# Norm scale and residual of a channel mixer applied once, in the last quarter, and VectorE's sums and low parts at group switches put in another order

## What is computed

```
hmlp = jax.nn.relu(rmsnorm(x, norm_mlp) @ w_up)
x = x + (hmlp * hmlp) @ w_down
...
y_prompt = rmsnorm(xp, norm_final)
```

## Time and profile before

| | |
|---|---|
| median of 3 runs | 2247.58 us (2243.97 to 2250.3) |
| the profiled execution: time, span | 2242.76 us, 2241.0 us |
| PE busy | 2157.6 us (96% of the span) |
| DVE busy | 1519.6 us (68%) |
| POOL busy | 1154.0 us (51%) |
| ACT busy | 667.8 us (30%) |

### The profile page before, as it was taken

How to read it: one execution, slowest core, us unless ns; L and a number is a source line. 1 busy time by engine, 2 the same in 40 slices (tenths; PEclk the granted TensorE clock), 3 DMA queues, 4 the chain that set the end, 5 groups by cost and what they waited for, 6 DMA issues and landing times.

```text
span 2241.0 us, 37284 instructions
## 1 busy us (share of the span) xinstructions
PE 2157.6 (96%) x14230; PEld 2129.1 (95%) x14230; DVE 1519.6 (68%) x1578; ACT 667.8 (30%) x850; POOL 1154.0 (51%) x785
## 2 busy tenths in 40 slices
PE   7999999999999999999999998979999999898998
PEld 6999999999999999999999998979999999898988
DVE  6576767165757667676757546477777678988856
ACT  4443434113223232323232202232222242433322
POOL 4556555342424334243424334458777778787761
PEclk9999999999999999999999999999999999999999
DMA  3212113421211112121212124423434554434322
GB/s 123 67 58 66 58 57 104 148 95 39 76 59 52 55 47 64 43 68 43 64 47 74 33 87 133 128 82 118 158 118 154 182 199 167 149 106 126 114 62 81
DMA packets 88609, 207.53 MB, mean 93 GB/s; under 512 B 8880, under 2 KB 14128, under 8 KB 87504
## 3 DMA queue, kind: packets, MB, share of 16 engines
q1 hardware_dynamic: 62992, 132.58, 18.8%
q10 hardware_dynamic: 25536, 73.83, 9.6%
HBM read 157.03 MB, written 49.34 MB: 92 GB/s over the span
## 4 chain that ended last, share of the span: by engine, by line
PE 76%; DVE 14%; issue 6%; ACT 3%; DMA 1%; DVEq 0%; POOL 0%; POOLq 0%; ACTq 0%; SPq 0%
PE ps L808 43%; PE ps L1031 21%; PE ps L1130 4%; DVE vt L1708 2%; PE ps L929 2%; DVE acc L1711 2%; DVE form_lo L1711 2%; PE ps L957 1%; DVE tmp L1711 1%; PE ps L975 1%; PE ps L978 1%; DVE snap L1711 1%; ACT vt L1140 1%; DVE xm_lo L1711 1%; PE ps L983 1%
## 5 line engine op out<-in xcount | busy, mean ns | idle before, releaser
L686 POOL TENSOR_TENSOR w_hi<-w_raw,ones 128x512 fp32r<-128x512 f32 x218 | 267.6, 1228 | 831.7 <-PE ps L808 803.6
L808 PE MATMUL ps<-u_hi,w_hi 128*128 128x364 f32 x1560 | 348.1, 331 | 16.9 <-POOL w_lo L689 9.6
L689 POOL TENSOR_TENSOR w_lo<-w_raw,w_hi 128x512 fp32r<-128x512 f32 x218 | 348.8, 1600 | 17.1
L808 PE MATMUL ps<-u_hi,w_lo 128*128 128x364 f32 x1560 | 344.8, 329 | 0.0
L808 PE MATMUL ps<-u_lo,w_hi 128*128 128x364 f32 x1560 | 344.3, 329 | 0.0
L808 PEld LDWEIGHTS ps<-u_hi,w_hi 128*128 128x128 f32 x1560 | 271.1, 189 | 19.4 <-issue 10.7
L808 PEld LDWEIGHTS ps<-u_lo,w_hi 128*128 128x128 f32 x1560 | 271.7, 188 | 0.0
L808 PEld LDWEIGHTS ps<-u_hi,w_lo 128*128 128x128 f32 x1560 | 271.6, 188 | 0.0
L1031 PE MATMUL ps<-form_hi,hi 128*128 128x274 f32 x784 | 168.9, 298 | 28.6 <-DVE small L1711 17.0
L1031 PE MATMUL ps<-form_hi,w_hi 128*128 128x274 f32 x776 | 164.0, 293 | 6.2 <-DVE small L1711 5.8
L1031 PE MATMUL ps<-form_lo,hi 128*128 128x274 f32 x784 | 167.5, 296 | 0.0
(11 more groups left out here) (286 smaller groups left out, 4510.9 us busy)
## 6 DMA issues: line engine op xcount, KB each, us to landing
w_raw<-in_w SPq DMA_DIRECT2D x290, 256.0 KB, 2.6
stage<-hid_forms SPq DMA_DIRECT2D x42, 548.0 KB, 3.9
rstd<-in_w SPq DMA_DIRECT2D x42, 256.0 KB, 2.6
hid_forms<-acc ACTq DMA_DIRECT2D x12, 822.0 KB, 6.6
bc<-out_rows ACTq DMA_DIRECT2D x8, 1092.0 KB, 6.1
hid_forms<-stage ACTq DMA_DIRECT2D x6, 1096.0 KB, 4.4
hid_forms<-acc ACTq DMA_DIRECT2D x6, 1096.0 KB, 4.4
acc<-in_x_t SPq DMA_DIRECT2D x8, 546.0 KB, 8.0
```

The costliest lines, as they stand in the source:

```text
L686: nc.gpsimd.tensor_tensor(w_hi[:, c, :], w_raw[:, c, :], one, ALU.mult).then_inc(s_whi, 1)
L689: nc.gpsimd.tensor_tensor(w_lo[:, c, :], w_raw[:, c, :], w_hi[:, c, :].bitcast(F32), ALU.subtract).then_inc(s_wlo, 1)
L808: mm = nc.tensor.matmul(slots[slot][:, t, :], w, r(k)[:, t * TW:(t + 1) * TW], start=(k == 0 and n == 0), stop=(k == last_k and n == 2))
```

## The change

The diff, cut to its core:

```diff
-ADDS = 8
+ADDS = 4
...
+    rings = [tmp[:, 2, 0:LAST_W], tmp[:, 2, LAST_W:2 * LAST_W], small[:, 0:LAST_W]]
...
+    def ring(q):
+
+        n = 2 * FORMS * DOWN_GROUPS + KB + q
+        return rings[n % STAGES], h_in[n % STAGES], 16 * (n // STAGES) + 16
...
-        def residual(first):
-            sp.dma_start(acc[:, first:first + 4, :], x2_d[first:first + 4].rearrange("j p c -> p j c"))\
-                .then_inc(g_in[first // 4], 16)
-
...
                 if q >= LAST_BANKS:
-                    pe.wait_ge(f_prod, q - LAST_BANKS + 1)
+                    pe.wait_ge(f_prod, 2 * (q - LAST_BANKS) + 1)
...
+        def residual(q):
+
+            lo, hi = LAST_TILES[q // KB]
+            dst, inc, count = ring(q)
+            act.dma_start(dst[:, 0:hi - lo], x2_d[q % KB, :, lo:hi]).then_inc(inc, 16)
+
+        act.wait_ge(o_st, 16 * KB)
+        act.wait_ge(v_lo, PRODUCTS)
+        act.wait_ge(h_add, ADDS * 4 * (DOWN_GROUPS - 1))
+        for q in range(STAGES):
+            residual(q)
 
         def final(t, n):
             lo, hi = LAST_TILES[t]
             q = KB * t + n
             act.wait_ge(f_acc, q + 1)
+            if q + STAGES < KB * TILES:
+                residual(q + STAGES)
...
-            if r == 3 and step == 3 and v <= DOWN_GROUPS:
-                staged_lo(v, B22)
...
-            if r == 0 and step == 0 and v > 1:
-                staged_lo(v - 1, T4)
+            if v <= DOWN_GROUPS:
+                f = {(2, 5): B11, (3, 0): T1, (3, 1): T2, (3, 3): B21, (3, 4): T3}.get((r, step))
+                if f is not None:
+                    staged_lo(v, f)
+            else:
+                first = {(2, 5): 0, (3, 0): 2, (3, 1): 4, (3, 2): 6}.get((r, step))
+                if first is not None:
+                    last_lo(first)
+            if v > 1 and r == 0 and step in (1, 2):
+                staged_lo(v - 1, (B22, T4)[step - 1])
...
+        def direct(group, r, product, n, half, part, count, over):
+
+            mm_done(group, r, product)
+            dve.wait_ge(s_q, QUARTERS * (4 * group + r) + max(count, over))
+            tt(as2(acc[:, n, (FIRST, SECOND)[half]]), bank(group, r, product), as2(part), ALU.add, s_q)
...
-            tt(tmp[:, 2, lo:hi], ps[:, q % LAST_BANKS, 0:hi - lo], tmp[:, 3, lo:hi], ALU.mult, f_prod)
-            dve.wait_ge(f_prod, q + 1)
-            tt(acc[:, n, lo:hi], acc[:, n, lo:hi], tmp[:, 2, lo:hi], ALU.add, f_acc)
+            x2, inc, count = ring(q)
+            y = acc[:, n, lo:hi]
+            tt(y, ps[:, q % LAST_BANKS, 0:hi - lo], y, ALU.add, f_prod)
+            dve.wait_ge(f_prod, 2 * q + 1)
+            tt(y, y, tmp[:, 3, lo:hi], ALU.mult, f_prod)
+            dve.wait_ge(f_prod, 2 * q + 2)
+            dve.wait_ge(inc, count)
+            tt(y, y, x2[:, 0:hi - lo], ALU.add, f_acc)
```

More of the change, by code:

```diff
@@ L2240, in partials @@
             mm_done(group, r, P6)
+            if isinstance(group, int) and group >= UP_GROUPS:
+                dve.wait_ge(s_q, QUARTERS * u)
             dve.wait_ge(s_snap, u + 1)
@@ L2370, in _ @@
             partials(group, r)
+            operands(group, r, 1)
             for stored_hid, count in hid_free(group, r):
@@ L2389, in mixer_add @@
                 tt(acc[:, n, FIRST], acc[:, n, FIRST], part, ALU.add, h_add)
[L2390 to L2398 removed]
+            dve.wait_ge(h_add, ADDS * (u - 4 * UP_GROUPS - 4) + done)
@@ new lines, in _ @@
+        group = UP_GROUPS
+        for r in range(4):
+            u = 4 * group + r
+            operands(group, r, 0)
+            partials(group, r)
+            for j in range(2):
+                dve.wait_ge(h_st[j], 32 * 6 + (32 if r >= 2 else 0))
+            operands(group, r, 1)
+            direct(group, r, P2, 2 * r, 0, snap1[:], 2, 0)
+            operands(group, r, 2)
+            direct(group, r, P7, 2 * r + 1, 1, snap4, 2, 0)
+            quarter(group, r, P7, snap2[:], snap2[:], 1)
+            operands(group, r, 3)
+            direct(group, r, P3, 2 * r, 1, snap4, 2, 3)
+            operands(group, r, 4)
+            direct(group, r, P4, 2 * r + 1, 0, snap2[:], 5, 4)
+            operands(group, r, 5)
```

65 lines of the change are left out of this document (17 added, 48 removed).

## The result

The changed kernel takes 2252.84 us in the median of 20 runs (2248.66 to 2259.62); the kernel before, beside it, 2245.15 us in 20 runs (2238.6 to 2250.3). The ratio is 1.0033, 95% interval 1.0026 to 1.0041: slower by 7.7 us, just above the 6.7 us that the prediction took as the least that can be told from no change. The profiled execution of the changed kernel has a span of 2249.8 us, 8.8 us more than before's 2241.0, and the same mean granted clock, 0.987. VectorE (DVE) is busy 1447.6 us instead of 1519.6 and POOL 1120.7 instead of 1154.0: 72 and 33 us of their busy time are gone, and the kernel is slower.

What follows compares the result with a forecast made beforehand. PE, busy 96% of the span, was taken as the bound. Stops +3.1, clock +0.8, POOL +3.0 and tail +1.9 sum to +8.8 us: 2247.6 + 8.8 = 2256.4 us on the median, range 2239.5 to 2267.

Steps and rivals of the forecast that it cites:

- (a): Likeliest, chance 0.45: stops move from r=3 to next group's start, last quarter pays; +9 us, +4 to +14.
- Stops in r = 3: Before P1 in units 15, 19, 23, 27: all four PE stops vanish, giving back 17.0 us.
- New stop before P1: In r=0 at units 16, 20, 24: PE waits 5.0 us each, 15.0 in all, for 5.3 before.
- New stop before P6: In r=0: PE stops of 3.3 (unit 16), 1.4 (20) and 4.2 us (24), 8.9 in all.
- Before the last quarter: PE's stop ahead of the last quarter grows to 2.5 us, for 0.9, as block 4's low part moves later.
- Stops together: Net of PE's new stops, less the 23.3 us of stops before the change: +3.1 us.
- Low clock: PE's stretches at the lower clock behind stops, five before, cost 0.8 us more.
- POOL in the first tile: Last quarter's first tile: POOL, meeting a third DVE instruction and starting later, costs PE 3.0 us (0 to 4.5).
- Tail: Last five blocks: one more 0.35 us DVE instruction each delays the last sum of squares, +1.9 us.
- (b): Rival, chance 0.15: the chain into P6 is hidden at the group switches; -2.6 us, no measurable change.
- (c): Rival, chance 0.18: every link of the chains at its low end; -8.0 us, 2239.6.
- (d): Rival, chance 0.22: links at their high end, landings 4.6 and more, longer P1 and P6 stops; +18 us, 2265.6.

Runs made afterwards that it cites:

- The two experiments on two links: Changed kernel with B22's low part back in r = 3: 2234.78 us; changed kernel with ACT's rounding of T4 moved later: 2234.86 us.
- e8: Changed kernel with ACT's rounding of T4 at step 2, B21's low parts a step earlier, T3's at step 3, B22's at step 5: 2226.67 us.
- the quarter alone: Changed kernel with the low parts in the old order, so only the last quarter's scale and residual are new: 2234.77 us.
- the order alone: Kernel before with only the new order of low parts; multiplications, additions and residual as before: 2268.89 us.
- e7: Changed kernel with most low parts at old places, T2's at r = 3 step 2, T4's later, ACT's rounding of T4 at step 2: 2227.14 us.

## Why the prediction was right

It said +8.8 us, 2256.4 on the median of the three runs shown; the medians differ by 7.7 and the spans by 8.8. The likeliest case, (a), holds, within its range, and the mechanism it named, stops that move from r = 3 to the start of the next group, is in the trace. That the spans differ by just 8.8 is luck: the stops came out 2.3 us lower than its sum, clock, POOL and tail 1.0, 1.1 and 1.0 higher, and -0.8 lies where it had no term.

- **Stops in r = 3, 17.0 us go**: they went, all four.
- **New stop before P1, 5.0 us each, 15.0**: 4.42, 4.29, 4.67, in all 13.4. Every link was where the prediction put it. The mis-sized ones, in unit 20: B22's first low part 1.25 us, not 1.8 and below the lower bound of 1.45, beside a POOL that stood idle there (7.69 us before 1952.33); T4's second half 3.85 us from issue to ACT's rounding, not 4.1. The two experiments on two links show the chain.
- **New stop before P6, 8.9 in all (3.3, 1.4, 4.2)**: P5 and P6 together 2.76, 0.23 and 5.25, in all 8.2. In unit 16 it stands before P5 and not P6: ACT waited 4.30 us for B21's second half, whose slot T2's first low part frees (also moved behind the partial sums), and P5's weights are queued behind it. The prediction followed only the chain to P6. In unit 24 the place is right. ACT's timeline there, T3's second half and then the copy:

```profile
2033.90 1.12 ACT L1134 ACTIVATE form_hi<-stage 128x1096 fp32r<-128x1096 f32 x1 [3.91 <-DMA stage<-hid_forms]
2034.93 0.61 ACT L1134 ACTIVATE snap<-ps 128x548 f32<-128x548 f32 x1
```

  Its slot was freed by B21's first low part, 2.3 us (4.59 for two from 2028.12), the high bound; the load took 3.5 us, inside the bounds. What B21's place costs is shown by e8: with it one step earlier, the stop is 1.02.
- **Before the last quarter 2.5**: 2.24, with 0.17.
- **Stops together +3.1**: +0.8, 2.3 too high. **Low clock +0.8**: +1.8. I had costed the clock by the number of stretches, and they are five as before; but the two at unit 24 cost 2.5 and 2.9 us, the other three 1.6 to 1.7. (The prediction's own terms for before, 1.7 + 2.1 and three of 1.7, make 8.9, not its 8.6; measured 8.5.)
- **POOL in the first tile +3.0 (0 to 4.5)**: +4.1 in these two executions, of the size given, but mis-split. The prediction put most of it on the third instruction and "some" on the late start. Against the kernel before, POOL starts 4.0 us later beside PE (3.5 us ahead, not 7.5), runs 1.2 us longer, and 1.0 us of slack behind its last chunk is gone; its 28 instructions took 38.4 us and 38.8 before. The 17.3 us for six chunks, from which it had POOL losing ground to PE, hold 1.3 us of waiting for transfers; without them a block's two chunks take 5.3 us of POOL, less than PE's 5.59. Other pairs give the instruction some part: 1.3 to 1.8 us by the medians, 2.2 by the profiles (48.75 against 46.55), 1.0 for the quarter alone (45.66 against 44.63), whose POOL starts 6.7 us ahead; the order alone, with the late start and without the instruction, has 47.16. Since two executions of one kernel differ by 2.5 us here, the split is argued, not shown. POOL's 28 instructions took 2.6 us more than without the instruction. The estimate by the exclusive lock of the Trainium skill's "SBUF — State Buffer", "Who interferes with whom", was 4.8 us, that by partial overlap 0 to 3.2, and the second is the nearer here.
- **Tail +1.9**: +2.9. The mechanism is shown (the same kernel without that instruction has 24.27 us, and the kernel before 24.26), the size was short by 1.0. The five instructions of 0.38 are there. The prediction counted only these. Ahead of them the tile's first blocks are late too: the stop of 0.46 us at the second norm and block 19's own third instruction put the reciprocal 13.57 us behind the tile's first matmul where it was 12.48, and ACT's square of the last block comes 0.3 us later (0.46 against 0.16 of waiting). That the transfers are hidden holds for all but one: block 16's, the last tile's first, is 0.83 us late, and the running sum behind it is what the second norm waits for. All the kernels with three instructions in that block have such a wait of 0.7 to 0.8 us and a stop of 0.3 to 0.5 at the second norm; the two kernels without the addition have neither.

The rivals: (b) fails because the P5 and P6 stops are 8.2 us; its reason against, late landings in bursts, holds (3.5/4.4/8.1 us min, median and max after, 3.4/4.1/7.9 before). (c) needed all links low: B22's was, B21's was not. (d) needed landings of 4.6 and more at P1; in unit 20 it was 3.9. What the prediction did not see is how much lay in the other half: it took no separate term for what the 74 us off DVE shorten, and the last quarter alone is a gain of 12 us, the order a loss of 18 in its presence and 22 without it.

## What to carry to other kernels

When an instruction is moved behind a wait, follow what its completion starts on other queues: here a stage slot, a load, a rounding, and the weight copies queued behind it in ScalarE's order. It was not the moved 2.5 us of VectorE's work that cost, but the 10 us from P6's end to P1's weights, and an edit on ScalarE, not on VectorE, undid the loss as well.

Time the halves of a change apart before judging it: 12 us gained and 18 lost look like a small loss. And ask of a stop not only how long it is but what clock follows: 24 us of stops brought 10 us of low clock with them, 12 to 13 us brought 3.3 to 8.0, and 7 to 8 us of shorter ones brought from none to 3.4.

When two engines feed one stage, look which of them sets its end before a longer stage is called slower: the first tile is 2.5 us shorter in the profile of e7 in which TensorE comes to it 2.0 us later, and ends at the same time.

Work placed ahead of time belongs where the engine waits for its producer, block by block, not where it is already behind: one block's behind each block of the middle tile, it lost 3.7 us to e7; behind the first three blocks, where VectorE waits, it lost nothing, though no gain in time is shown either.
